# Gated-linear output projection in rows, residual sums of the last projection on VectorE, and norm scaling by pairs of tiles

## The reference

```python
def first_block(...):
    ...
        sh1, sc1, g1, sh2, sc2, g2 = jnp.split(mod, 6, axis=-1)
        ...
        x = x + g1 * _rmsnorm(y, norm_g[l, 1])
        h = _rmsnorm(x, norm_g[l, 2]) * (1.0 + sc2) + sh2
        y = _conv_ffn(h, w_up[l], conv_w[l], conv_b[l], w_down[l])
        x = x + g2 * _rmsnorm(y, norm_g[l, 3])

def gla_mixer(...):
    ...
    return (o.astype(x.dtype) * jax.nn.silu(g)) @ w_out

def second_block(...):
    ...
        x = layer_norm(DEEPNORM_ALPHA * x + y, ln_g[layer], ln_b[layer])
```

## Time and profile before

| | us |
|---|---|
| median of 3 runs | 786.86 |
| lowest, highest | 785.42, 787.11 |
| the profiled execution | 786.95 |
| its span, first to last instruction | 785.2 |
| PE busy | 751.5 |
| DVE busy | 528.7 |
| ACT busy | 394.9 |
| POOL busy | 121.3 |

### The profile page before, as it was taken

The page is one execution under the profiler, slowest core; times in us unless marked ns, Lnnn a source line. Parts: engine busy times, 40 slices in busy tenths (PEclk is TensorE's granted clock), DMA queues, the critical chain, the costliest instruction groups (busy, mean ns, idle before and its releaser), DMA issues. The chain is left out here.

```text
span 785.2 us, 14371 instructions
## 1 busy us (share of the span) xinstructions
PE 751.5 (96%) x6044; PEld 732.4 (93%) x6044; DVE 528.7 (67%) x770; ACT 394.9 (50%) x555; POOL 121.3 (15%) x100
## 2 busy tenths in 40 slices
PE   8899989999898999999999999999989999999996
PEld 7889889899897999999999999999989999999995
DVE  5879978765868687778656556926685556556544
ACT  4195454555353555454444347627445555555633
POOL 0040000000521100000002150000025655333000
PEclk9999999999999999999999999979999999999999
DMA  8975575464355356554565524523437653333101
GB/s 355 417 291 215 215 268 187 190 259 171 108 177 199 115 208 210 173 200 157 209 247 210 211 90 180 184 88 108 145 124 246 201 185 135 134 109 119 44 1 54
DMA packets 20954, 140.10 MB, mean 178 GB/s; under 512 B 2357, under 2 KB 2997, under 8 KB 4890
## 3 DMA queue, kind: packets, MB, share of 16 engines
q1 hardware_dynamic: 20458, 137.28, 48.2%
q0 software_dynamic: 432, 1.90, 0.7%
HBM read 138.12 MB, written 1.05 MB: 177 GB/s over the span
## 5 line engine op out<-in xcount | busy, mean ns | idle before, releaser
L1593 PE MATMUL res<-hhi,whi 128*128 128x256 f32 (+1 forms) x1120 | 322.9, 288 | 5.3 <-DVE hlo L1071 2.9
L1035 DVE TENSOR_TENSOR wlo<-raw,whi 128x2048 fp32r<-128x2048 f32 (+3 forms) x102 | 230.0, 2256 | 142.9 <-ACT whi L647 138.3
L1595 PE MATMUL res<-hlo,whi 128*128 128x256 f32 (+1 forms) x1120 | 317.8, 284 | 0.0
L1594 PE MATMUL res<-hhi,wlo 128*128 128x256 f32 (+1 forms) x1120 | 317.8, 284 | 0.0
L647 ACT ACTIVATE whi<-raw 128x2048 fp32r<-128x2048 f32 (+3 forms) x102 | 190.1, 1865 | 132.5 <-issue 100.2
L1593 PEld LDWEIGHTS res<-hhi,whi 128*128 128x128 f32 (+1 forms) x1120 | 214.6, 192 | 7.2 <-issue 5.5
L1594 PEld LDWEIGHTS res<-hhi,wlo 128*128 128x128 f32 (+1 forms) x1120 | 214.4, 191 | 0.3
L1595 PEld LDWEIGHTS res<-hlo,whi 128*128 128x128 f32 (+1 forms) x1120 | 214.3, 191 | 0.2
L559 POOL TENSOR_TENSOR sq<-sq 128x512 f32<-128x512 f32 x6 | 14.9, 2482 | 293.7 <-ACT sq L853 168.5
L1593 PE MATMUL res<-uhi,whi 128*128 128x256 f32 x176 | 49.3, 280 | 1.0 <-ACT y L854 1.0
L1594 PE MATMUL res<-uhi,wlo 128*128 128x256 f32 x176 | 49.2, 280 | 0.0
(11 more groups left out here) (331 smaller groups left out, 1242.0 us busy)
## 6 DMA issues: line engine op xcount, KB each, us to landing
raw<-in_wts SPq DMA_DIRECT2D x97, 1024.0 KB, 4.9
raw<-in_w_ada SPq DMA_DIRECT2D x16, 1024.0 KB, 4.9
shared<-in_w_ada SPq DMA_DIRECT2D x6, 1024.0 KB, 12.6
gates<-in_wts SPq DMA_DIRECT2D x3, 1024.0 KB, 15.4
raw<-in_wts SPq DMA_DIRECT2D x4, 768.0 KB, 7.3
y<-in_w_ada SPq DMA_DIRECT2D x2, 1024.0 KB, 10.3
x<-in_xT SPq DMA_DIRECT2D x2, 512.0 KB, 4.5
ln_rows<-in_ln_rows POOLq DMA_DIRECT2D x1, 1024.0 KB, 7.9
```

The source lines that it names most:

```text
L1035: nc.vector.tensor_tensor(lo[:, 0:b], raw[RAW_OF["w", c] % RAW][:, 0:b], hi[:, 0:b].bitcast(f32), ALU.subtract).then_inc(lo_ready, 1)
L1593: mm(out, ah, bh, start=first, stop=False)
L1594: mm(out, al, bh, start=False, stop=False)
L1595: return mm(out, ah, bl, start=False, stop=last)
```

## The change

- **Norms n2 and n4.** The gate columns are computed earlier, and ACT's drains multiply by them while they copy (`n2`'s drain becomes two instructions of one tile each). DVE multiplies `y` by `rstd` a pair of tiles at a time and does all four pair sums; POOL's two sums go. Behind `n4` the low halves are interleaved with them. `ada(19)`, the columns that need it and the loading of the root's table move; 36 unread products on PE become 24.
- **Gated-linear projection.** It is computed in rows. The residual `xe` goes into the banks as identity products; chunk `SK - 1` has a split buffer of its own, `wgo`. The first half of the tokens (`t = 0`) is finished before the second, and its layer norm (`rows_normed`, as at the end of the program, with rows loaded into `gv` by POOL) runs beside the second half's products. PE turns the normed rows back to feature-major by transposes (`hidden`) into `pS` and `pT`, which ACT and DVE split from there. The sums with a matrix of 1/1024, the centring and POOL's part of norm `n5` are gone. `SK` and `SK + 1` run one after the other.
- **Last projection.** The 16 identity products go. DVE adds the residual rows as it drains, with the sum as accumulator output (`row_add`); ACT squares what DVE has written. POOL multiplies the residual rows by `ALPHA` in two instructions instead of eight.

```diff
+    return 2 if c == SK - 1 else 1
...
-    if GOUT <= c < SV or SWA <= c < SWA + 12:
+    if SK <= c < SV or SWA <= c < SWA + 12 or c >= SOUT:
...
+CHUNK_MARK[GOUT + 1] = RESULT_MARK[FIRST_RESULT[GOUT + 3]]
+CHUNK_MARK[GOUT + 2] = CHUNK_MARK[GOUT + 3]
...
+            wgo = sb("wgo", [P, 2, CW], f32r, at=st)
...
+            if c == SK - 1:
+                return wgo[:, 0, :], wgo[:, 1, :]
...
+            return {NC - 1: SOUT - 1, SK - 1: GOUT - 1, SK + 2: GOUT}.get(c, c - SPL)
...
-                    add_pair("n2")
...
+                if c - 1 == GG:
+                    pool.wait_ge(o_done, 2)
+                    pool.dma_start(gv[:, :, :], ln_rows5_d).then_inc(rows5_in, 16)
+                if SV <= c - 1 < SV + 2:
+                    t = c - 1 - SV
+                    pool.wait_ge(h_transposed, 4)
+                    nc.gpsimd.tensor_scalar(x_rows[:, t, :], x_rows[:, t, :], ALPHA, None, ALU.mult).then_inc(x_ready, 1)
...
-                    if j == 3:
-                        load_root()
...
-                    nc.scalar.activation(y[:, 2 * j:2 * j + 2, :].rearrange("p a b -> p (a b)"), ps[:, :], ACT.Copy
-                                         ).then_inc(drained_act, 1)
+                    act.wait_ge(pcol_ready, 5)
+                    for i in range(2):
+                        nc.scalar.activation(y[:, 2 * j + i, :], ps[:, T * i:T * i + T], ACT.Copy,
+                                             scale=pcol[:, 1, 2 * j + i:2 * j + i + 1]).then_inc(drained_act if i else act_self, 1)
+                    act_count[0] += 1
                     if j == 2:
+                        load_root()
                         high(c + 2)
...
+                if b == GOUT:
                     ps = result(FIRST_RESULT[b])
                     for t in range(2):
-                        nc.scalar.activation(z[:, t, T * j:T * j + T], ps[:, T * t:T * t + T], ACT.Copy,
-                                             accum_out=zs[:, t, j:j + 1]).then_inc(drained_act if t else act_self, 1)
+                        row_sum(ps[:, T * t:T * t + T], t, 0, T, 0).then_inc(drained_act if t else act_self, 1)
                     act_count[0] += 1
+                    load_root()
+                if b == GOUT + 1:
+                    row_sum(result(FIRST_RESULT[b])[:, 0:T], 0, T, T, 1).then_inc(drained_act, 1)
+                    act.wait_ge(z_shift, 1)
+                    row_squares(z[:, 0, 0:512], 0, 0, 3).then_inc(z_squared, 1)
+                if b == GOUT + 2:
+                    ps = result(FIRST_RESULT[b])
+                    row_sum(ps[:, :], 0, 512, 512, 2).then_inc(z_summed, 1)
+                    row_squares(ps[:, :], 0, 512, 4).then_inc(drained_act, 1)
+                    row_root(0, 0)
+                if b == GOUT + 3:
+                    row_sum(result(FIRST_RESULT[b])[:, 0:T], 1, T, T, 1).then_inc(drained_act, 1)
+                    act.wait_ge(z_shift, 2)
+                    row_squares(z[:, 1, 0:512], 1, 0, 3).then_inc(z_squared, 1)
+                    high(SK)
+                    hidden_high(0)
+                    ps = result(FIRST_RESULT[b] + 1)
+                    row_sum(ps[:, :], 1, 512, 512, 2).then_inc(z_summed, 1)
+                    row_squares(ps[:, :], 1, 512, 4).then_inc(drained_act, 1)
+                    row_root(1, 0)
+                    hidden_high(1)
+                    high(SK + 1)
...
-                if b == UP - 2:
-                    dve.wait_ge(ada_used, ada_done(19))
-                    own(nc.vector.tensor_tensor(pcol[:, 1, :], mod[:, 16:24], col("norm_g", 8, 8), ALU.mult))
-                    own(nc.vector.scalar_tensor_tensor(pcol[:, 2, :], mod[:, 32:40], 1.0, col("norm_g", 16, 8),
-                                                       ALU.add, ALU.mult))
+                if b == ZG + 4:
+                    dve.wait_ge(ada_used, ada_done(11))
+                    nc.vector.tensor_tensor(pcol[:, 1, :], mod[:, 16:24], col("norm_g", 8, 8), ALU.mult).then_inc(pcol_ready, 1)
                 if b == UP - 1 or b == GK - 1:
-                    n, which = ("n2", 1) if b == UP - 1 else ("n4", 3)
+                    n = "n2" if b == UP - 1 else "n4"
                     norm_rstd(n)
                     dve.wait_ge(drained_act, RESULT_DRAIN[FIRST_RESULT[b] + results_of(b) - 1][1])
                     for i, j in enumerate(PAIRS):
-                        for k in (2 * j, 2 * j + 1):
-                            ins = nc.vector.scalar_tensor_tensor(y[:, k, :], y[:, k, :], pcol[:, which, k:k + 1], rstd[:, :],
-                                                                 ALU.mult, ALU.mult)
-                            if i == 1 and k % 2:
-                                ins.then_inc(y_scaled[n], 1)
-                            else:
-                                own(ins)
-                        if i != 1:
-                            nc.vector.tensor_tensor(x[:, 2 * j:2 * j + 2, :], x[:, 2 * j:2 * j + 2, :],
-                                                    y[:, 2 * j:2 * j + 2, :], ALU.add).then_inc(scaled[n], 1)
-                        if n == "n4" and i == 2:
-                            low_pair(0)
+                        own(nc.vector.tensor_tensor(y[:, 2 * j:2 * j + 2, :], y[:, 2 * j:2 * j + 2, :],
+                                                    rstd[:, None, :].to_broadcast([P, 2, T]), ALU.mult))
+                        if n == "n4" and i:
+                            low_pair(i - 1)
+                        nc.vector.tensor_tensor(x[:, 2 * j:2 * j + 2, :], x[:, 2 * j:2 * j + 2, :],
+                                                y[:, 2 * j:2 * j + 2, :], ALU.add).then_inc(scaled[n], 1)
                     if n == "n4":
-                        for i in (1, 2, 3):
-                            low_pair(i)
+                        low_pair(3)
                 if b == UP - 1:
+                    ada(ADA_AFTER[UP])
+                    dve.wait_ge(ada_used, ada_done(ADA_AFTER[UP]))
+                    own(nc.vector.scalar_tensor_tensor(pcol[:, 2, :], mod[:, 32:40], 1.0, col("norm_g", 16, 8),
+                                                       ALU.add, ALU.mult))
...
+                if b == GOUT:
+                    low(c + 2)
+                if b == GOUT + 1:
+                    dve.wait_ge(drained_act, RESULT_DRAIN[FIRST_RESULT[b]][1])
+                    shift_of(0)
+                if b == GOUT + 2:
+                    dve.wait_ge(rows5_in, 16)
+                    dve.wait_ge(xe_ready, 1)
+                    rows_normed(0, 0, gv, x_rows, x_rows_ready)
+                if b == GOUT + 3:
+                    dve.wait_ge(drained_act, RESULT_DRAIN[FIRST_RESULT[b]][1])
+                    shift_of(1)
+                    low(SK)
+                    hidden_low(0)
+                    rows_normed(1, 0, gv, x_rows, x_rows_ready)
+                    hidden_low(1)
+                    low(SK + 1)
...
+                def row_add(ps, t, a, n, at):
+                    return nc.vector.tensor_tensor_reduce(out=z[:, t, a:a + n], in0=ps, in1=x_rows[:, t, a:a + n], op0=ALU.add,
+                                                          op1=ALU.add, scale=1.0, scalar=0.0, accum_out=zs[:, t, at:at + 1])
+
+                if b == SOUT:
+                    low(c + 2)
+                    dve.wait_ge(x_ready, 2)
+                if SOUT <= b < SOUT + 2:
+                    ps = result(FIRST_RESULT[b])
+                    own(row_add(ps[:, 0:T], 0, T * (b - SOUT), T, b - SOUT))
+                    row_add(ps[:, T:2 * T], 1, T * (b - SOUT), T, b - SOUT).then_inc(drained_dve, 1)
+                if b == SOUT + 1:
+                    dve.wait_ge(drained_dve, RESULT_DRAIN[FIRST_RESULT[b]][1])
+                    for t in range(2):
+                        shift_of(t)
+                    dve.wait_ge(rows_in, 16)
+                if b >= SOUT + 2:
+                    t = b - SOUT - 2
+                    row_add(result(FIRST_RESULT[b])[:, :], t, 512, 512, 2).then_inc(z_summed, 1)
+                    dve.wait_ge(z_summed, t + 3)
+                    nc.vector.engine_nop().then_inc(drained_dve, 1)
+                    rows_normed(t, 2, ln_rows, result_rows, out_ready)
...
-                        warm(36)
+                        warm(24)
...
+                        pe.wait_ge(xe_ready, 1)
+                        ps = bank(r)
+                        for t in range(2):
+                            residual(ps, T * t, t, (0, 1))
+                        wh, wl = weights(c)
+                        for k in range(KT):
+                            pe.wait_ge(go_lo, k // 2 + 1)
+                            for t in range(2):
+                                last = token_product(ps, T * t, t, k, gohi, golo, wh, wl, False, k == KT - 1 and t == 1)
+                        last.then_inc(product_done, 1)
+                    if c == GOUT + 1:
+                        for t in range(2):
+                            ps = bank(r + 1 + 2 * t)
```

(32 more changed lines are left out.)

281 lines of the change are left out of this document (94 added, 187 removed).

## The result

The changed kernel takes **772.46 us** (median of four runs, 771.61 to 774.38) where the kernel before takes 786.34 (785.42 to 787.11): a ratio of 0.9827, 95% interval 0.9805 to 0.9849. That is faster, as forecast, and by 13.9 rather than 10.3 to 10.9; the lower end of the range, 773.2, lies 0.7 above the median. The profiled execution is the slowest of the four, 774.38 with a span of 772.6, against 786.95 and 785.2 before. Between the two traces lie 12.6. Four more executions of the changed kernel (the first experiment) had a median of 774.19, inside the forecast's range.

What follows compares the result with a forecast made beforehand. PE was taken to bound the kernel, holding 35% of the chain of waits, with gains where it does other than weight products. Four places, -3.4 - 2.7 + 0.0 - 4.8 = -10.9, gave 776.05, median 776.0; range 773.2 to 779.8.

Steps and rivals of the forecast that it cites:

- n2 and n3: Norms behind the first output projection and the feed-forward's start: moved `ada(19)` and pairwise multiplies gain 3.4 us, bounds -2.4 and -3.9.
- The floor of unread products: At n2, PE's unread products run 6.3 us, to 242.1, limiting how early the sums of new squares can follow.
- n4: Norm behind the feed-forward layer: 24 unread products instead of 36 still decide PE's next chunk; -2.7 us, bounds -2.0 and -3.1.
- an extra table load at `DOWN`: ACT's table load in the down projection: lies beside products with more than one chunk (5.7 us) of cover.
- Gated-linear projection: Projection plus the layer norm behind it: `SK` starts at 586.0 against 586.09, so 0.0 us, bounds -1.0 and +3.5.
- The wait for the last low half: In the gated-linear projection: PE wants this half at 555.65 and gets it 1.0 us later.
- the start of the first half's transposes: In the gated-linear projection: PE reaches them at 575.1, their rows are ready at 573.5, 1.6 us of cover.
- the second half's norm: Behind the gated-linear projection: ACT and DVE come to it late by 0.4 us.
- End: Last projection and final norm: no bank wait, no identity products on PE; -4.8 us, bounds -4.2 and -5.1.
- the first (a dearer norm in the middle): Rival: the row norm behind the gated-linear projection costs more than its model; +2.5 us, 778.5, chance 0.12.
- second: Rival: the gain at n2 and n3 is lost to a late load behind `ada(19)`'s buffer; +3.4 us, 779.4, chance 0.05.
- The third: Rival: PE's clock falls to half for 9 us around the sparse stretch before `SK`; +4.5 us, 780.5, chance 0.03.

Runs made afterwards that it cites:

- the first experiment: Changed kernel and kernel before, both run again without an edit: changed 774.19 us (771.71 to 776.29), before on that chip 785.88.
- its relative: Kernel before with only ACT's table load for norm n4 moved from the drains at `DOWN + 2` to chunk `DOWN`'s start: 785.26 against 785.88 us, ratio 0.9989.

## Why the forecast was right and wrong

- **n2 and n3**, forecast -3.4: right, -3.0 to -3.6 against three traces of before, and for the reasons given; n3's L1066 stands 3.55 earlier. The floor of unread products held (they end at 240.5, the squares' sums follow), but DVE's chain lies just under it: three unread products fewer gave 0.12.
- **n4**, forecast -2.7: right, -2.81 against -2.68 for the twelve products alone.
- **"an extra table load at `DOWN`"**, costed at nothing, as lying "beside products, with more than one chunk (5.7) of cover": this is the step that failed. It was not an extra load but the one from `DOWN + 2`, moved, and I asked only whether its new place was covered. I never priced its old place, where it stood ahead of the drains that PE's next bank waits for. It is worth 1.3 to 1.4 by the runs, and 1.05 between the two traces (1.29 for the wait that is gone, less 0.24 for a slightly wider pitch of 1585 products). It is also most of what separates the forecast from the trace: -12.6 for -10.9. With it in the sum the forecast would have been 774.7 and the range 771.9 to 778.5. No group of rows ahead of the prediction shows that place, since I had looked for PE's waits at the norms alone.
- **Gated-linear projection**, forecast 0.0: right. The wait for the last low half was put at 1.0 and is 1.09; the start of the first half's transposes had cover; the second half's norm began 0.4 behind its drain's sum at most; from PE's start to `SK` 35.7, forecast 586.0 - 550.45 = 35.6. The bounds of -1.0 and +3.5 were wider than needed. That it came so near is partly luck, since this place had no row of its own kind.
- **End**, forecast -4.8: right, -4.99 in the trace and +5.06 in the run with the identity products back. DVE's slack ahead of the last drain was 0.29.
- **Clock, and scatter.** The forecast held the half-clock spells of before fixed. They are not: -1.22 in the head and +1.24 in the attention, which cancel between these two traces but not between executions. The changed kernel's eight timed runs spread over 4.7, where 15 of the kernel before, timed beside the second four, spread over 2.3; the eight have their middle at 773.3. The traces give, without the clock, -3.55 - 1.05 - 2.81 - 0.36 + 0.30 + 0.05 - 4.99 - 0.20 = -12.6, so 786.3 - 12.6 = 773.7. The median of the first four, 772.46, lies another 1.2 lower, within that spread; that it fell below 773.2 is in part luck, for the repeat's 774.19 lies above it. It is not half-clock time alone: the other three of the four had spans of 770.7, 769.8 and 770.6 at mean clocks of 0.986, 0.988 and 0.986, so they were 1.9 to 2.8 shorter than the profiled one (0.989) with as much time at half clock or more. A spell of 10.2 in place of 13.7 and the 1.15 under "Open" would make such a difference together; without traces of them that is a guess.

Of the rivals, the first (a dearer norm in the middle) and second did not come: PE's first transposes, at 567.53, have no wait. The third did not come in the two traces of the changed kernel but is real: it was priced at half a us for each us at half clock and costs 0.3 to 0.4, probably since part of a spell falls on waits and small products. Its argument against, that the gap of 2.21 had not lowered the clock, held in two of three traces that have the gap.

**Open:** in five of the eleven traces of changed kernels PE reaches n2 1.15 earlier, counted from the first product of the branches (47.2 for 48.35); there a wait for `hlo` (L1287) ahead of the first output projection is missing. None of the three traces of the kernel before and its relative is without that wait, so it may be a part of the gain, or of the wider spread, that the forecast has no term for; I did not test what decides it.

## What to carry to other kernels

When an instruction is moved, price the place it leaves as well as the place it goes to: look at who waited behind it, on its own engine and on the next. A chain of norm between two layers is best filled by ordering the next layer so that the part that needs only half of the tokens comes first; that gave 2.9 us where taking unread products away at two other norms gave 0.26. And before a microsecond is explained, take a second trace of the same kernel.

## What the runs showed of the chip

- PE busy 100% with products of 16 columns came to a granted clock of 0.50, that is 1.2 of 2.4 GHz, 2.5 to 5.2 us behind the first of them, in all 13 traces without unread products among them; in the one trace with an unread product of full size behind every eight it stayed at 1.00.
- An idle time of 4.85 ahead of dense work brought 6.8 at 0.50; filled but for 1.28 and 0.84, it brought none in seven traces and 3.4 in one. The gap of 2.21 of the kernel before brought none in two traces and 3.4 in one.
- A wait of PE cost 0.27 more than its length (1.02 cost 1.29, 1.10 cost 1.37, from start to start, at a pitch of 0.12).
- DVE's sum of a bank and a row with its accumulator read takes 0.69 + 0.08; a pair of tiles times a broadcast row 0.69, where two single tiles with a column and a row took 1.00, and 1.40 beside POOL's sum.
